# Normed projections into eight PSUM banks, and another order of loads in the expert routing

## What is computed

```python
def rms_norm(x, g):
    y = x * lax.rsqrt(jnp.mean(x * x, axis=-1, keepdims=True) + 1e-6)
    return y * g
...
# block 1: the attention's output, gated per column
x = x + g1l * (o @ attn_out_w)
# blocks 0 and 1: routing; moe_ec picks rows by softmax(h @ router_w) and gathers them from h
h = rmsnorm(x, norm2_w) * (1.0 + sc2) + sh2
x = x + g2 * moe_ec(h, router_w, w1, w3, w2)
# third block: three projections whose product is normed before it is added
x = x + rms_norm(merged @ w_out, g_mix_post)
x = x + rms_norm(mem_out @ w_mem_o, g_mem_post)
x = x + rms_norm(hidden @ w_ffn_out, g_ffn_post)      # this sum is the output
```

## Time and profile before

| what | us |
| --- | --- |
| median of 3 runs | 3928.37 (3925.65 to 3932.37) |
| the profiled execution, its own time | 3933.86 |
| its span, first to last instruction | 3932.1 |
| PE busy | 3461.1 (88% of the span) |
| DVE busy | 2324.5 (59%) |
| ACT busy | 1679.6 (43%) |
| POOL busy | 1509.0 (38%) |
| mean granted TensorE clock | 0.926 |

### The profile page before, as it was taken

One profiled execution on the slowest core, in us unless ns is written; L12 is line 12 of the kernel. 1 busy time (PEld: TensorE's weight loads), 2 busy tenths in 40 slices (PEclk: granted clock), 3 DMA queues, 4 the chain that ended last, 5 costly groups with the idle time before them and its releaser, 6 DMA issues. The chain is left out here.

```text
span 3932.1 us, 45064 instructions
## 1 busy us (share of the span) xinstructions
PE 3461.1 (88%) x17417; PEld 2550.9 (65%) x17417; DVE 2324.5 (59%) x2866; ACT 1679.6 (43%) x2539; POOL 1509.0 (38%) x796
## 2 busy tenths in 40 slices
PE   5999997998959999958995999996988996759997
PEld 2778877987846666645664555553776644538875
DVE  1037765874289999945655999996028842233211
ACT  3111223443147777732542777775323311442212
POOL 3323335640156666621013666663423201214432
PEclk9979998999879999979996999998978998779998
DMA  5423444432379999935005999995112233122140
GB/s 209 146 93 124 169 162 138 131 111 99 120 284 379 383 390 382 343 117 193 1 7 202 368 378 377 378 378 209 61 61 73 89 105 115 43 77 100 65 145 22
DMA packets 306353, 710.05 MB, mean 181 GB/s; under 512 B 16144, under 2 KB 63084, under 8 KB 303836
## 3 DMA queue, kind: packets, MB, share of 16 engines
q1 hardware_dynamic: 299312, 685.98, 47.3%
q0 software_dynamic: 6144, 20.98, 2.5%
q10 hardware_dynamic: 684, 0.21, 0.0%
HBM read 653.59 MB, written 53.54 MB: 180 GB/s over the span
## 5 line engine op out<-in xcount | busy, mean ns | idle before, releaser
L133 POOL TENSOR_TENSOR weights_low<-ring,weights_high 128x1024 fp32r<-128x1024 f32 (+2 forms) x210 | 498.7, 2381 | 1135.6 <-ACT weights_high L126 1128.1
L579 PE MATMUL ps<-h_parts,weights_high 128*128 128x512 f32 (+2 forms) x2528 | 741.6, 379 | 39.8 <-POOL weights_low L133 33.3
L579 PEld LDWEIGHTS ps<-h_parts,weights_high 128*128 128x128 f32 (+1 forms) x2528 | 463.4, 191 | 148.9 <-POOL weights_low L133 36.7
L579 PE MATMUL ps<-h_parts,weights_low 128*128 128x512 f32 (+2 forms) x1264 | 474.9, 376 | 0.0
L1907 DVE TENSOR_TENSOR more_low<-area,more_high 128x1024 fp32r<-128x1024 f32 x192 | 330.5, 1760 | 0.0
L1874 ACT ACTIVATE weights_high<-ring 128x1024 fp32r<-128x1024 f32 x256 | 271.3, 1061 | 135.6 <-PE ps L1807 92.9
L126 ACT ACTIVATE weights_high<-ring 128x1024 fp32r<-128x1024 f32 (+1 forms) x158 | 161.5, 1040 | 356.6 <-PE ps L579 234.2
L1874 ACT ACTIVATE more_high<-area 128x1024 fp32r<-128x1024 f32 x256 | 271.8, 1062 | 86.0 <-PE ps L1807 85.8
L1907 DVE TENSOR_TENSOR weights_low<-ring,weights_high 128x1024 fp32r<-128x1024 f32 x192 | 300.2, 1617 | 2.7 <-ACT weights_high L1874 2.7
L1778 POOL TENSOR_TENSOR more_low<-area,more_high 128x1024 fp32r<-128x1024 f32 x64 | 243.7, 3808 | 110.6 <-ACT more_high L1874 110.6
L579 PE MATMUL ps<-weights_high,h_parts 128*128 128x512 f32 (+2 forms) x832 | 258.5, 390 | 20.1 <-POOL weights_low L133 20.1
(11 more groups left out here) (432 smaller groups left out, 7301.2 us busy)
## 6 DMA issues: line engine op xcount, KB each, us to landing
ring<-in_moe_w SPq DMA_DIRECT2D x96, 2048.0 KB, 10.9
area<-in_moe_w SPq DMA_DIRECT2D x96, 2048.0 KB, 10.3
ring<-in_ada_w SPq DMA_DIRECT2D x24, 2048.0 KB, 8.7
ring<-in_ssd_in_w SPq DMA_DIRECT2D x12, 2048.0 KB, 10.9
ring<-in_w_in SPq DMA_DIRECT2D x11, 2048.0 KB, 7.9
ring<-in_w_ffn_in SPq DMA_DIRECT2D x10, 2048.0 KB, 7.8
area<-x_dram SPq DMA_DIRECT2D x12, 1024.0 KB, 5.0
ring<-in_ssd_out_w SPq DMA_DIRECT2D x4, 2048.0 KB, 10.1
```

The lines of the kernel that those rows point to most:

```text
L133: pool.tensor_tensor(lo, views[k][:, ks, cols], hi, ALU.subtract).then_inc(self.low_p, 1)
L579: mm = pe.matmul(out, a, b, start=start and n == 0, stop=stop and n == 2)
```

## The change

In `project_add`, the second half of the columns goes to PSUM banks 4 to 7, so no bank is used twice in a stage. ACT no longer copies. In the normed calls it squares each half tile straight from PSUM, the first half's four tiles between the halves and the second half's as each bank closes; DVE adds the two sums and the epsilon per tile (`mean`), ACT takes a root per tile (`root`), and DVE scales both halves from PSUM into one of two buffers and adds the tile to X. ACT starts each normed call with a one-column square root, ahead of its first weight block. In the gated call DVE multiplies from PSUM. In the last call SP stores each row tile when its sum is done, and the stage `store` is gone.

In `dispatch`, SP issues the spread rows ahead of the store of the summed rows. DVE makes the latent gain row itself, in one instruction after the inverse root, and POOL makes only the context gain (block 0). DVE writes its modulated tiles to buffers of their own and so waits neither for `kept` nor for the transposes; POOL still works in place, waits as before, and also for DVE's gain. SP waits for `kept` at the end of the stage. The branch of `project_add` for weights that are not split is deleted; no call used it.

```diff
-        o = st.sb("product", [P, n_t, D])
...
+        spread = st.sb("row_weights", [P, D])
+        o = st.sb("product", [P, 2, D])
+        junk = st.sb("squares", [P, HALF])
+        ss = st.sb("mean_squares", [P, 3, NL])
...
+            if out is not None:
+                for j in range(NL):
+                    sp.wait_ge(summed, j + 1)
+                    sp.dma_start(out[j * P:(j + 1) * P, :], X[:, j, :]).then_inc(stored, 16)
+                sp.wait_ge(stored, 16 * NL)
...
-                    if n == 1 and q == 0:
-                        pe.wait_ge(copied, j + 1)
+                for j in range(NL):
                     for k in (2 * q, 2 * q + 1):
-                        mm = products(pe, ps[:, j, :], tuple(x[:, k, i * P:(i + 1) * P] for x in hT),
+                        mm = products(pe, ps[:, 4 * n + j, :], tuple(x[:, k, j * P:(j + 1) * P] for x in hT),
...
+            def square(n, j):
+                act.wait_ge(ring.done, closed(n, j))
+                act.drain()
+                act.activation(junk, ps[:, 4 * n + j, :], ACT.Square, scale=float(D) ** -0.5,
+                               accum_out=ss[:, n, j:j + 1]).then_inc(squared, 1)
+            def root(j):
+                act.wait_ge(eps_in, j + 1)
+                act.activation(ss[:, 2, j:j + 1], ss[:, 2, j:j + 1], ACT.Sqrt).then_inc(rooted, 1)
+            if gate is None:
+                act.activation(junk[:, 0:1], env.ones[:, 0:1], ACT.Sqrt)
             m = 0
             for n in range(2):
-                if parts:
-                    for q in range(kd // 2 - 1):
-                        m = ring.cut_after(act, cuts, views, m, m0 + n * per + q)
-                    m = ring.cut_after(act, cuts, views, m, m0 + n * per + kd // 2 - 1)
-                for j in range(n_t):
-                    act.wait_ge(ring.done, m0 + n * per + per - n_t + j + 1)
-                    act.activation(o[:, j, n * HALF:(n + 1) * HALF], ps[:, j, :], ACT.Copy).then_inc(copied, 1)
-            if norm is not None:
-                act.drain()
-                for j in range(n_t):
-                    act.drain()
-                    act.activation(junk, o[:, j, :], ACT.Square, scale=float(D) ** -0.5,
-                                   accum_out=ss[:, j:j + 1]).then_inc(squared, 1)
-                act.wait_ge(eps_in, 1)
-                act.activation(ss, ss, ACT.Sqrt).then_inc(rooted, 1)
+                for q in range(pairs):
+                    m = ring.cut_after(act, cuts, views, m, m0 + n * per + q)
+                if gate is None and n == 0:
+                    for j in range(NL):
+                        square(0, j)
+            if gate is None:
+                square(1, 0)
+                for j in range(1, NL):
+                    square(1, j)
+                    root(j - 1)
+                root(NL - 1)
...
+            if gate is not None:
                 for n in range(2):
                     h = slice(n * HALF, (n + 1) * HALF)
-                    for j, i in enumerate(tiles):
-                        dve.wait_ge(copied, n * n_t + j + 1)
-                        dve.tensor_tensor(o[:, j, h], o[:, j, h], spread[:, gate[0](i), h], ALU.mult)
+                    for j in range(NL):
+                        dve.wait_ge(ring.done, closed(n, j))
+                        dve.tensor_tensor(o[:, j % 2, h], ps[:, 4 * n + j, :], spread[:, h], ALU.mult)
                         dve.drain()
-                        dve.tensor_tensor(X[:, i, h], X[:, i, h], o[:, j, h], ALU.add)
-            else:
-                dve.wait_ge(squared, n_t)
-                dve.tensor_scalar(ss, ss, EPS, None, ALU.add).then_inc(eps_in, 1)
-                dve.wait_ge(rooted, 1)
-                dve.reciprocal(ss, ss)
+                        dve.tensor_tensor(X[:, j, h], X[:, j, h], o[:, j % 2, h], ALU.add)
+                return
+            def mean(j):
+                dve.wait_ge(squared, NL + j + 1)
+                dve.scalar_tensor_tensor(ss[:, 2, j:j + 1], ss[:, 0, j:j + 1], EPS, ss[:, 1, j:j + 1], ALU.add, ALU.add).then_inc(eps_in, 1)
+            mean(0)
+            for j in range(NL):
+                if j + 1 < NL:
+                    mean(j + 1)
+                dve.wait_ge(rooted, j + 1)
+                r = ss[:, 2, j:j + 1]
+                dve.reciprocal(r, r)
                 dve.drain()
-                for j, i in enumerate(tiles):
-                    dve.scalar_tensor_tensor(o[:, j, :], o[:, j, :], ss[:, j:j + 1], spread[:, 0, :], ALU.mult, ALU.mult)
-                    dve.drain()
-                    dve.tensor_tensor(X[:, i, :], X[:, i, :], o[:, j, :], ALU.add)
+                for n in range(2):
+                    h = slice(n * HALF, (n + 1) * HALF)
+                    dve.scalar_tensor_tensor(o[:, j % 2, h], ps[:, 4 * n + j, :], r, spread[:, h], ALU.mult, ALU.mult)
+                dve.drain()
+                dve.tensor_tensor(X[:, j, :], X[:, j, :], o[:, j % 2, :], ALU.add).then_inc(summed, 1)
...
             sp.dma_start(rw, env.ins["moe_router_w"][layer].rearrange("(k p) e -> p k e", p=P)).then_inc(w_in, 16)
-            sp.dma_start(env.sum_dram[layer][0:nt * P, :].rearrange("(t p) d -> p t d", p=P), X[:, 0:nt, :]).then_inc(kept, 16)
             sp.dma_start(weight, env.ins["norm2_w"][layer].partition_broadcast(P)).then_inc(rows_in, 16)
             for u in range(len(segs)):
                 for t, q in ((gain, 4), (bias, 3)):
                     sp.dma_start(t[:, u, :], env.mod_dram[layer, u, q * D:(q + 1) * D].partition_broadcast(P)).then_inc(rows_in, 16)
+            sp.dma_start(env.sum_dram[layer][0:nt * P, :].rearrange("(t p) d -> p t d", p=P), X[:, 0:nt, :]).then_inc(kept, 16)
             for c in range(CHUNKS):
                 feed.load(sp, layer, 0, c)
             for j in range(half_nt):
-                for sem, i in ((by_dve, j), (by_pool, half_nt + j)):
+                for sem, i, rows_ in ((by_dve, j, modulated[j]), (by_pool, half_nt + j, X[:, half_nt + j, :])):
                     sp.wait_ge(sem, j + 1)
-                    sp.dma_start(env.xn_dram[layer][i * P:(i + 1) * P, :], X[:, i, :]).then_inc(stored, 16)
+                    sp.dma_start(env.xn_dram[layer][i * P:(i + 1) * P, :], rows_).then_inc(stored, 16)
             sp.wait_ge(stored, 16 * nt)
-        def modulate(eng, i, done):
-            u = int(i >= NL)
-            if done is by_dve:
-                eng.scalar_tensor_tensor(X[:, i, :], X[:, i, :], rstd[:, i:i + 1], gain[:, u, :], ALU.mult, ALU.mult)
-            else:
-                eng.tensor_scalar(X[:, i, :], X[:, i, :], rstd[:, i:i + 1], None, ALU.mult)
-                eng.drain()
-                eng.tensor_tensor(X[:, i, :], X[:, i, :], gain[:, u, :], ALU.mult)
-            eng.drain()
-            eng.tensor_tensor(X[:, i, :], X[:, i, :], bias[:, u, :], ALU.add).then_inc(done, 1)
+            sp.wait_ge(kept, 16)
 
         @block.gpsimd
         def _(pool):
             pool.memset(aff, -1.0).then_inc(cleared, 1)
             pool.wait_ge(rows_in, 16 * (1 + 2 * len(segs)))
-            for u in range(len(segs)):
-                pool.tensor_scalar(gain[:, u, :], gain[:, u, :], 1.0, None, ALU.add)
+            if len(segs) > 1:
+                pool.tensor_scalar(gain[:, 1, :], gain[:, 1, :], 1.0, None, ALU.add)
                 pool.drain()
-                last = pool.tensor_tensor(gain[:, u, :], gain[:, u, :], weight, ALU.mult)
-            last.then_inc(gains, 1)
-            pool.drain()
+                pool.tensor_tensor(gain[:, 1, :], gain[:, 1, :], weight, ALU.mult)
+                pool.drain().then_inc(gain_1, 1)
             pool.wait_ge(kept, 16)
             pool.wait_ge(inverse, 1)
             pool.wait_ge(turned, 2 * nt)
+            pool.wait_ge(gain_0, 1)
             for j in range(half_nt):
-                modulate(pool, half_nt + j, by_pool)
+                i = half_nt + j
+                u, row = int(i >= NL), X[:, i, :]
+                pool.tensor_scalar(row, row, rstd[:, i:i + 1], None, ALU.mult)
+                pool.drain()
+                pool.tensor_tensor(row, row, gain[:, u, :], ALU.mult)
+                pool.drain()
+                pool.tensor_tensor(row, row, bias[:, u, :], ALU.add).then_inc(by_pool, 1)
...
-            dve.wait_ge(kept, 16)
-            dve.wait_ge(gains, 1)
-            dve.wait_ge(turned, 2 * nt)
+            dve.wait_ge(rows_in, 16 * (1 + 2 * n))
+            dve.scalar_tensor_tensor(gain[:, 0, :], gain[:, 0, :], 1.0, weight, ALU.add, ALU.mult)
+            dve.drain().then_inc(gain_0, 1)
             for j in range(half_nt):
-                modulate(dve, j, by_dve)
+                if j == 2:
+                    dve.wait_ge(gain_1, 1)
+                dve.scalar_tensor_tensor(modulated[j], X[:, j, :], rstd[:, j:j + 1], gain[:, 0, :], ALU.mult, ALU.mult)
+                dve.drain()
+                dve.tensor_tensor(modulated[j], modulated[j], bias[:, 0, :], ALU.add).then_inc(by_dve, 1)
...
```

(4 more changed lines are left out.)

80 lines of the change are left out of this document (22 added, 58 removed).

## The result

| | kernel before | changed kernel |
| --- | --- | --- |
| median | 3931.22 us (3925.65 to 3932.37, 5 runs) | 3898.61 us (3896.23 to 3908.91, 5 runs) |
| the profiled execution, own time | 3933.86 | 3905.97 |
| its span | 3932.1 | 3904.2 |
| mean granted TensorE clock | 0.926 | 0.927 |

The changed kernel takes 0.9927 of the time before, with an interval of 0.991 to 0.9944. The forecast was 3902.5, the range 3894 to 3911; the direction was right and the median lies 3.9 under the forecast. The two profiled executions are 27.9 apart. The median of before is 2.9 above the 3928.37 that the forecast started from, because two more runs of the kernel before came in.

What follows compares the result with a forecast made beforehand. PE, busy 88% of the span, was taken as the bound, so only stretches where it stands still could pay. 3 x 6.0 + 4.2 + 0.6 + 2.6 + 0.5 = 25.9 off 3928.37 gave 3902.5 us, range 3894 to 3911.

Steps and rivals of the forecast that it cites:

- Tails: Ends of the three normed projections: last sum 14.18 us after tile 0's closing instead of 21.65, gaining 7.5 each.
- Heads: Starts of the three normed projections: table load and small root ahead of ACT's first weight block shift everything by 1.5 us.
- Rival (a): More gained: barrier hides the heads' load (4.5 us) or stores do not end block 1's routing (2.9); chance 0.15.
- (b): Heads of normed projections cost 3.0 us each, by a pause behind the load or slower PE start; 3907.0, chance 0.13.
- the forecast's own last sign: In ffn: the forecast is wrong altogether if PE's stretch of 125 us changes.
- The output's store: End of the kernel: only the last 512 KB land behind the last sum, 3.0 us instead of 7.2, gaining 4.2.
- The gated projection: Its end: DVE no longer behind ACT's copy, ending 1.46 us after the last closing, gaining 0.6.
- Block 1's routing: Routing stage of block 1: DVE finishes earlier, the stores then end the stage, gaining 2.6 us; bounds 0 to 5.5.
- Rival (c): Routing: rows at the queue's head delay block 1's stores, or DVE and POOL collide in block 0; 3905 to 3907, chance 0.10.
- Block 0's routing: Routing stage of block 0: small instruction 1.9 us less, new gain adds 1.36, net 0.5; bounds -1.4 to 2.4.
- rival (e): Experts: PE waits in each of 32 passes; 3934.5 at 1.0 us each; chance 0.02, plus 0.04 for 3921.7.
- The total: Whole kernel: terms sum to 25.9 us, taken from the earlier median of 3928.37, giving 3902.5.

Runs made afterwards that it cites:

- one_root: Changed kernel with one mean, root and inverse for all four tiles behind the last square in each normed projection; median 3910.81 us, ratio 0.9952 to the kernel before.
- root_late: Changed kernel with the one-column root and its table load moved behind ACT's first group of weight blocks; median 3897.37 us, ratio 0.9918 to the kernel before.
- store_whole: Changed kernel with the output stored by one 2 MB transfer behind the last sum; median 3907.09 us, ratio 0.9935 to the kernel before.
- old_routing: Changed kernel with the old `dispatch`, its loads, gains and stores as before; median 3909.14 us, ratio 0.9941 to the kernel before.
- stores_before_chunk: Changed kernel with the sixth chunk of expert weights issued behind the stores of normed rows in the routing; median 3905.86 us, ratio 0.9932 to the kernel before.
- chunk_behind_gather: Changed kernel with the sixth weight chunk issued at the experts' start, behind a wait for the first two gathers; median 3897.83 us, ratio 0.9915 to the kernel before.
- pe_early: root_late plus eight products of no use on PE at the start of each normed projection; median 3891.95 us, ratio 0.9901 to the kernel before.

## Why the prediction was right, step by step

- **Tails, 7.5 forecast:** 7.8 measured (21.66 to 13.89). The start of scaling was forecast at 2.57 and is 2.46, the pitch 2.99 and is 2.92. The terms given for DVE's first inverse add up to 2.40 before any gap and were written as 2.3; it starts at 2.21, because a closing and the square behind it follow without the 0.10 that I added for a drain. DVE is late next, as forecast; with one_root its later start moves the end.
- **Heads, 1.5 forecast:** 1.4 measured, in three stages alike, and given back in full by root_late. Rival (a), a load hidden by the barrier, is out, and so is (b) at its price of 3.0: no drain shows, and a longer slow start of PE shows in ffn alone, at 0.7. I had taken PE's stretch as fixed ("PE's 125 us follow without slack"). It is not: in mix and mem the clock rose 4.3 and 3.8 us behind the first product instead of 5.9 and 5.1, which gave 0.7 and 0.6 back, and in ffn 5.2 instead of 3.9, which took 0.7. With this, mix is 7.8 - 1.4 + 0.7 = 7.1 for 7.03 measured, mem 7.8 - 1.4 + 0.6 = 7.0 for 7.00, ffn 7.8 - 1.4 - 0.7 + 4.2 = 9.9 for 9.93. So the step that called PE's stretch fixed was wrong, and by the forecast's own last sign ("wrong altogether if PE's stretch of 125 us changes") it did change, from 125.2 to 125.8. It cost the forecast little because the three shifts of the clock add up to only 0.6; that is luck.
- **The output's store, 4.2:** 4.2 (7.2 to 2.99); 7.0 again in store_whole.
- **The gated projection, 0.6:** 0.62.
- **Block 1's routing, 2.6:** 2.59 in the pair of profiles and 2.2 in old_routing, with SP the last to arrive, as forecast; stores_before_chunk and chunk_behind_gather show that without this bound the stage would be 3.2 to 3.9 shorter. Rival (c), stores delayed by the rows ahead, did not occur.
- **Block 0's routing, 0.5:** the step was right and under-sized, 0.6 to 1.1. The stage of this execution still came out 0.35 longer, through a first part whose scatter of 1.9 is larger than the term. That -0.35 lies within the stated -1.4 to 2.4 is luck: this bound was for a collision of DVE and POOL, and the first part was not in it.
- **Experts, rival (e):** 574.74 and 571.98 against 575.06 and 572.17. No pass is slower: from the second pass on, SP's loads of one pass follow those of the pass before by 34.8 in both kernels.
- **The total:** the terms sum to 25.9, and the changed stages gained 26.8. The medians are 32.6 apart. The 3.9 between forecast and median are 0.9 from the terms, 1.1 from the drift of the unchanged stretches, and 1.9 from a step of the sum that did not hold: I took the 5.5 between the profiled execution and the median of before as constant, and the changed kernel's profiled execution is 7.4 above its median. Where those 7.4 lie no trace shows. They are not the stretch of 401 or 408, since the profiled execution has the short form. All that the runs show is that, of the changed kernel's five executions, the three of 3896 to 3899 us have a mean granted clock of 0.930 to 0.932, and the two of 3906 and 3909 us 0.927 and 0.925. A forecast of the median carries a scatter of this size whatever its terms are.

## What to carry to other kernels

An instruction ahead of the first one of a chain that the whole machine waits for costs its full length, here 1.4 us in each stage; put table loads and other preparations behind the first piece of work, where the engine stands still anyway. When a faster engine makes a stage end with a transfer, look at what is queued ahead of that transfer, but also at what the moved transfer meets next: the chunk that was put behind the stores took back 3.5 of 3.9, most of it by meeting the gather, and kept out of both it cost nothing. Where PE has to stand still for a few us before a long stretch, products of no use in that time are worth trying.

## What the hardware showed that I had not expected

PE's clock level in the first few us of a stage is worth more than the 1.4 us of the head: eight products of no use gained 2.27, 1.96 and 1.76 us in three stages. The granted clock stayed at 1.00 through idle times of 3.1 and 1.5 us in mix, and was at 0.50 when PE resumed after 8.0 us in the changed kernel (7.2 in ffn). It is not the idle time alone: in ffn of pe_early it fell although PE had stood still for only 2.3 us. And the same code in an unchanged stretch took 401 to 403 us in nine of the profiled executions and 408 in three, with the granted clock over some 20 us at 0.66 to 0.85 and then 1.00 in the one case, and at 0.50 and then 0.65 to 0.67 in the other.
